# Moving the sample tile to the front of a hybrid decoder layer, routing each tile as it is finished, and adding the residual in the expert stage

## The reference

```
proj = x @ w_in
A half: causal conv + silu on q, k, v; gated delta rule in chunks over a state (per head 128x128); gated RMSNorm
B half: trailing means over 2/4/8/16 positions, a linear map per group
mix = concat(A, B) @ w_out ; h = LayerNorm(ALPHA*x + mix)
lg, le = h @ w_rg, h @ w_re               # 4 groups, 8 experts in each
top-1 group, top-2 experts in it, softmax weights
y = LayerNorm(ALPHA*h + sum over chosen experts of weight * (silu(h Wg) * (h Wu)) Wd)
```

## Time and profile before

| | us |
|---|---|
| device time, median of 3 runs | 1169.77 (1169.17 to 1171.09) |
| the profiled execution, its device time | 1168.77 |
| its span | 1167.0 |
| PE busy | 971.8 |
| DVE busy | 393.2 |
| ACT busy | 173.5 |
| POOL busy | 226.7 |
| stage 2, mixing, begins | 342 |
| stage 3, routing, begins | 712 |
| stage 4, experts, begins | 756.15 |
| stage 5, last LayerNorm, begins | 1108.5 |

### The profile page before, as it was taken

One profiled execution on the slowest core, in us unless ns is written; L12 is line 12 of the kernel. 1 busy time (PEld: TensorE's weight loads), 2 busy tenths in 40 slices (PEclk: granted clock), 3 DMA queues, 4 the chain that ended last, 5 costly groups with the idle time before them and its releaser, 6 DMA issues. The chain is left out here.

```text
span 1167.0 us, 13262 instructions
## 1 busy us (share of the span) xinstructions
PE 971.8 (83%) x5403; PEld 547.1 (47%) x5403; DVE 393.2 (34%) x737; ACT 173.5 (15%) x357; POOL 226.7 (19%) x238
## 2 busy tenths in 40 slices
PE   6999999999887999999988762049999999995583
PEld 4666666655445666666765422023333333331231
DVE  0434332586005554545542344201111111110056
ACT  1222233111021111111100000011111111110012
POOL 1011111220013222221113100611121211201047
PEclk9999999999888999999998875569999999998787
DMA  6011110202425011110031007757999999996094
GB/s 259 19 37 37 37 37 32 61 34 56 142 76 184 10 46 37 45 45 31 24 112 51 28 1 279 276 161 291 378 422 418 414 411 387 395 391 235 0 332 163
DMA packets 61323, 186.51 MB, mean 160 GB/s; under 512 B 22984, under 2 KB 36328, under 8 KB 51720
## 3 DMA queue, kind: packets, MB, share of 16 engines
q1 hardware_dynamic: 34640, 157.73, 35.3%
q0 software_dynamic: 8208, 19.09, 4.4%
q10 hardware_dynamic: 18416, 8.86, 2.7%
HBM read 164.15 MB, written 30.01 MB: 166 GB/s over the span
## 5 line engine op out<-in xcount | busy, mean ns | idle before, releaser
L359 PE MATMUL pj<-xT,wblk 128*128 128x384 f32 (+1 forms) x960 | 300.0, 474 | 18.3 <-DMA xT<-in_xt_dram 9.2
L359 PEld LDWEIGHTS pj<-xT,wblk 128*128 128x128 f32 x960 | 183.3, 192 | 129.8 <-issue 17.7
L1708 PE MATMUL e<-wgu_s,xgT 128*32 128x512 f32 x384 | 170.9, 598 | 0.0
L1708 PE MATMUL e<-wgu_a,xgT 128*32 128x512 f32 x768 | 114.7, 600 | 6.2 <-issue 3.2
L1708 PE MATMUL e<-wdn_a,acT 128*32 128x512 f32 x576 | 86.8, 592 | 0.7 <-ACT acT L1777 0.7
L1708 PE MATMUL e<-szT,acT 128*32 128x512 f32 x192 | 86.3, 592 | 0.0
L1694 PE MATMUL e<-cst,xg 128*128 128x128 f32 x200 | 28.7, 291 | 65.2 <-DMA xg<-h_dram,lst 48.4
L994 PE MATMUL b<-wout,yaT 128*128 128x512 f32 x144 | 69.7, 630 | 3.8 <-DVE yaT L1319 3.8
L1821 DVE SCALAR_TENSOR_TENSOR ac<-sg,lst,e 128x256 f32<-128x256 f32 x24 | 11.5, 480 | 171.2 <-ACT sg L1773 171.2
L1656 POOL DMA_INDIRECT picked_dram<-yo,lst x24 | 24.1, 1005 | 229.3 <-PE e L1694 185.0
L1708 PEld LDWEIGHTS e<-wgu_a,xgT 128*32 128x32 f32 x768 | 32.3, 111 | 75.9 <-issue 72.4
(11 more groups left out here) (321 smaller groups left out, 1248.4 us busy)
## 6 DMA issues: line engine op xcount, KB each, us to landing
wgu_a<-in_w_gate_up_dram SPq DMA_DIRECT2D x17, 2048.0 KB, 22.4
wdn_a<-in_w_down_dram SPq DMA_DIRECT2D x25, 1024.0 KB, 13.9
wgu_s<-in_w_gate_up_dram SPq DMA_DIRECT2D x8, 2048.0 KB, 15.6
qkvT<-in_w_gate_up_dram SPq DMA_DIRECT2D x8, 2048.0 KB, 19.4
wblk<-in_wcol_dram SPq DMA_DIRECT2D x20, 512.0 KB, 3.3
szT<-in_w_down_dram SPq DMA_DIRECT2D x8, 1024.0 KB, 18.1
picked<-picked_dram SPq DMA_DIRECT2D x8, 1024.0 KB, 5.7
h_dram<-h SPq DMA_DIRECT2D x9, 512.0 KB, 2.6
```

Source lines behind the costliest of these rows:

```text
L359: last = pe.matmul(pj[par][:, bank * 512:bank * 512 + m], wblk[par][:, k, :], xT[:, k, a:a + m], start=(k == 0), stop=(k == KT - 1))
L1708: last = pe.matmul(out[at, :], lhsT[:, at], theirs if j == GROUP - 1 else mine, start=start, stop=stop)
```

## The change

The tiles go in the order sample, prompt 0 to 7 (`ORDER`). The sample's states are loaded first, into rooms of their own (`st_s`); POOL scales them, and `sample_states` runs head by head in the second step, each with the same masked copy and the banks b3 and b4. Stage 3 goes: behind each tile's logits DVE chooses group and experts (`choose`), TensorE counts (`counts`) and DVE gives places (`place`) one step later, and POOL writes two scatters a tile. The weights of the expert stage are laid in the room of tiles that are finished, partly in steps 4, 7 and 9, and 12 MB behind the last product; the first gate/up slots are two in dead `qkvT` and three in turn. In stage 4 the gathered rows stay in four buffers (`NX = 4`) until the pass is put out, because `out_v` adds ALPHA times them, weighted by a fourth entry of the list; both halves are now DVE's. The order of overflow passes is worked out on DVE at pass 3. Stage 5 has no TensorE work: DVE adds the two rows, ACT takes the root, gain is split between DVE and POOL, bias is POOL's.

```diff
-            SAMPLE = PT
...
+            ORDER = [PT] + list(range(PT))
+            SAMPLE, LAST = 0, NT - 1
...
+                    for hh in range(H):
+                        sp.dma_start(st_s[hh], sdelta_d[0, :, hh].rearrange("s d e -> d s e")).then_inc(sst_in, 16)
+                    sp.dma_start(xct.rearrange("p n i -> p (n i)"), xct_d).then_inc(xc_in, 16)
+                    sp.dma_start(xc.rearrange("p n i -> p (n i)"), xc_d).then_inc(xc_in, 16)
...
+                        if i == 4:
+                            dead(3)
+                            load_own_gu(0)
...
+                            load_own_gu(1)
+                            e.wait_ge(ya_ready, 5)
+                            load_shared_dn(0)
+                        if a == LAST:
+                            dead(LAST)
+                            load_own_gu(2)
...
+                        if r == LAST:
+                            e.wait_ge(mix_done, NT)
+                            load_shared_gu(0)
+                            e.wait_ge(delta_out, 16)
+                            load_own_dn(0)
+                            load_own_dn(1)
+                            load_own_gu(3)
+                            load_own_dn(2)
+                            load_own_gu(4)
+                            load_shared_gu(1)
+                            load_shared_dn(1)
...
+                    pool.memset(on, 0.0).then_inc(cleared2, 1)
+                    pool.memset(xt[:, :], 0.0).then_inc(cleared2, 1)
+                    pool.memset(st, 0.0).then_inc(st_ready, 1)
...
+                        if a == SAMPLE:
+                            e.wait_ge(ks_raw, 1)
+                            for hh in range(H):
+                                pool.tensor_tensor(st_s[hh], st_s[hh], bc(eglast_s[:, :, hh], P), ALU.mult
+                                                   ).then_inc(scaled, 1)
...
+                        if r is not None and r >= 1:
+                            scatter(r - 1)
...
+                    scatter(LAST)
+                    e.wait_ge(listed, 16 * 2 * NT)
...
-                            if a < SAMPLE:
+                            if a == SAMPLE:
+                                sample_states(0)
+                            else:
...
+                        if a == SAMPLE:
+                            sample_states(1)
+                            mix(a, H + 2)
+                            sample_states(2)
+                            mix(a, H + 3)
+                            sample_states(3)
...
+                            if r >= 1:
+                                counts(r - 1)
...
-                        if a == SAMPLE:
-                            e.wait_ge(lg_ready, r + 1)
-                            for hh in range(H):
-                                sample_states(hh)
...
+                    e.wait_ge(lg_ready, NT)
+                    counts(LAST).then_inc(fixed, 1)
...
+                    def first_max(values, w, top, scratch, onehot):
+
+                        link(dve.tensor_reduce(top, values, AX.X, ALU.max))
+                        link(dve.scalar_tensor_tensor(out=scratch, in0=values, scalar=top, in1=w, op0=ALU.is_equal,
+                                                      op1=ALU.mult))
+                        link(dve.tensor_reduce(sm[:, :], scratch, AX.X, ALU.max))
+                        link(dve.tensor_scalar(onehot, scratch, sm[:, :], None, ALU.is_equal))
...
+                            if r >= 1:
+                                place(r - 1)
...
+                            choose(r)
...
-                        wait(e, xg_turned, q - 1)
-                        pool.indirect_dma_start(xg[q % 2][:, :], None, h_d,
+                        wait(e, yo_ready, 2 * (q - NX + 1))
...
-                    for q in range(3):
+                    for q in range(NX):
                         gather(q)
-                    for q in range(NPASS):
-                        if q + 3 < NPASS:
-                            gather(q + 3)
-                        if q >= 1:
-                            scatter(q - 1)
+                    for q in range(1, NPASS):
+                        scatter(q - 1)
+                        if q + NX - 1 < NPASS:
+                            gather(q + NX - 1)
...
-                def out_s(e, i, k):
-                    e.wait_ge(dn_done, i + 1)
-                    act.activation(yo[k][:, 0:512], b[6][:, :], ACT.Copy).then_inc(yo_ready, 1)
...
-                def out_v(e, i, k):
+                def out_v(e, i, k, rows, entry):
                     e.wait_ge(dn_done, i + 1)
-                    dve.tensor_copy(yo[k][:, 512:], b[7][:, :]).then_inc(yo_ready, 1)
+                    for half in range(2):
+                        c = slice(half * 512, (half + 1) * 512)
+                        dve.scalar_tensor_tensor(out=yo[k][:, c], in0=rows[:, c], scalar=entry.bitcast(F32),
+                                                 in1=b[6 + half][:, :], op0=ALU.mult, op1=ALU.add).then_inc(yo_ready, 1)
...
+                        if q == NA:
+                            overflow_order(e)
...
-            NB = 3
+            NB = 4
...
+                        pool.tensor_tensor(fin[k][:, hi], fin[k][:, hi], lng[:, hi], ALU.mult).then_inc(scaled_p, 1)
...
+                        pool.tensor_tensor(fin[k][:, :], fin[k][:, :], lnb[:, :], ALU.add).then_inc(out_ready, 1)
...
+                        dve.tensor_tensor(res[k][0:m, :], picked[k][0:m, 0:D], picked[k][0:m, D:], ALU.add
+                                          ).then_inc(summed, 1)
...
+                        dve.tensor_tensor(fin[k][:, lo], fin[k][:, lo], lng[:, lo], ALU.mult).then_inc(scaled_v, 1)
...
+                        link(dve.reciprocal(rstd[k][:, :], dev[k][:, :]))
+                        dve.scalar_tensor_tensor(out=shift[k][:, :], in0=mv[k][:, 0:1], scalar=-1.0, in1=rstd[k][:, :],
+                                                 op0=ALU.mult, op1=ALU.mult).then_inc(shift_ready, 1)
```

More of the change, by code:

```diff
@@ new lines, in build, with gu_rows, dn_rows @@
+        wdn_s = [dn_of(gates_of[:, k * DN:(k + 1) * DN]) for k in range(ND)]
+        kept = phase(whole)
+        gu_e_in = [kept(f"gu_e_in{k}") for k in range(EARLY)]
+        gu_a_in, dn_a_in = ([kept(f"{n}{i}") for i in range(NA)] for n in ("gu_a_in", "dn_a_in"))
+        gu_s_in, dn_s_in = ([kept(f"{n}{i}") for i in range(ND)] for n in ("gu_s_in", "dn_s_in"))
+        def gu_rows(expert):
+            return wgu_d[ds(expert, 1)].rearrange("a p k f -> (a p) k f")
+        def dn_rows(expert):
+            return wdn_d[ds(expert, 1)].rearrange("a p c d -> (a p) c d")
@@ L1024, in sample_states, with counts @@
                                              start=True, stop=True)
                         last.then_inc(ds_done, 1)
+                    def counts(r):
+                        e.wait_ge(both_ready, r + 1)
+                        pe.matmul(b[1][:, 64:64 + NE], C("strict"), both[:, :], start=True, stop=True)
+                        return pe.matmul(b[1][:, 64 + NE:64 + 2 * NE], C("ones"), both[:, :], start=True, stop=True)
                     def step(p, i, a, r):
-                        whole_tile = i is not None and i < SAMPLE
+                        whole_tile = i is not None and i != SAMPLE
@@ L1576, in build @@
+                            wait(e, gexp_ready, r)
+                            if r >= 1:
+                                place(r - 1)
+                            dve.tensor_tensor(logits[:, :], b[1][:, 0:G + NE], brt[:, :], ALU.add).then_inc(lg_ready, 1)
+                            e.wait_ge(lg_ready, r + 1)
+                            choose(r)
+                    steps(step)
+                    e.wait_ge(fixed, 1)
+                    place(LAST)
         with ExitStack() as c4:
@@ L1582, in build @@
             olst = sb("olst", [P, 4], I32, ctx=c4)
-            xg, xgT = two("xg", [P, D]), two("xgT", [P, KT, P])
+            NX = 4
+            xg = [sb(f"xg{k}", [P, D], ctx=c4)[:, :] for k in range(3)] + [rows_of[:, EARLY * GU:EARLY * GU + D]]
+            xgT = two("xgT", [P, KT, P])
             sg, ac, acT = two("sg", [P, FE]), two("ac", [P, FE]), two("acT", [P, FE // P, P])
```

883 lines of the change are left out of this document (395 added, 488 removed).

## The result

The changed kernel takes 1210.62 us (median of 4 runs, 1204.20 to 1213.87) against 1169.47 for the kernel before (measured once more, median of 4 now); the ratio is 1.0357, with a 95% interval of 1.0314 to 1.0401. That lies above the range given (1131 to 1192), and the likeliest case was no change. The profiled execution is the fastest of the four (1204.20, span 1202.4), so it is compared with the profiled execution of before (1168.77, span 1167.0): +35.4.

A forecast was written before the change was run, and what follows sets the result against it. TensorE was taken to bound mixing steps and expert passes, nearly idle from 712 to 778 us. Mixing, routing and start -42.5, passes +35.5, overflow residual +1.4, last stage +4 summed to -1.6: 1169.8 to 1168 us, range 1131 to 1192.

The forecast's parts named there:

- the likeliest case: Whole kernel: the forecast itself, sum -1.6 to 1168 us, own range 1158 to 1179, chance 0.35.
- (a): First two mixing steps: with the sample tile first no inverse to wait for, -10 of 10.7 us of waits.
- (b): Sample tile's second half: last step -17.8, state products behind it -13.0, second step +30 to 58 us; together -1.
- (c): Routing on DVE behind each step's logits: products taken 2.4 us late, mostly absorbed, +0.5 a step, +4 in all.
- The rival: Mixing steps: routing on DVE delays each step, the 2.4 us not absorbed, +15 over the sum, 1183 us; chance 0.10.
- the 36 that I had named as a sign of being wrong: Mixing steps: the prediction called itself wrong if steps run at 36 us.
- (d): Routing stage, last take to expert stage: 32.5 us instead of 62.45, -30; weights +1, bounds 0 and +8.
- (e): Start of the experts: first turn about 10 us after the stage begins instead of 16.4, -6.5, bounds 0 and -8.
- The expert passes: Gathers issued later with four buffers: light stalls 0.75, heavy 5.25 us, 42 less 6.5 of weight waits, +35.5.
- the lower clock behind them: Expert passes: stalls of 5 us may lower the clock, each costing up to 3 us; taken as 0, bound +18.
- The case that gathers land in time: Expert passes: a drained queue gives landings of 6.7 us, stalls 0 to 10 in all, 1133 to 1143 us; chance 0.25.
- The last stage: Sum without TensorE: first sum -6, POOL and DVE exclusion makes the period 5.4 us instead of 4.07, +10; net +4.

The follow-up runs named there:

- e_routing2: Changed kernel with group choice ahead of Y in the next step, expert choice at that step's end, scatters behind the next mask product: 1185.91 us, -24.7.
- e_five: Changed kernel with five buffers for gathered rows instead of four, so each gather is issued one pass earlier: 1168.00 us, -42.6.
- e_weightslate: Changed kernel, four buffers kept, with the next weights asked for only once POOL has issued the pass's gather: 1208.81 us, -1.8.
- e_last: Changed kernel's last stage with the sum on TensorE, whole gain on DVE, only bias on POOL, stores between loads: 1210.30 us, -0.3.
- e_shift: e_last with DVE's one-column shift using a scalar per row instead of a second tensor operand: 1202.13 us, -8.5 against the changed kernel.

## Why the prediction was wrong

**(a), (b) The sample tile first: right in the sum, 5 us too good, and in part by luck.** +20.7 to the first take against +20. The halves missed by 3 us each and cancelled: the first step lost 13.1 us (28.1 to 15.0), not 10, and the second took 61.2, not 58. In the second step the state rows' product alone took 10.6 us where 5 stood for it and its copy. In return, the row of 3.70 in the earlier trace rows holds the products of two heads and not of one, so the term 4 x 3.7 was counted twice; they took 10.1, partly at the lower clock, and the waits for DVE in it were 6.5 us, not 10.4. With routing out of the way (e_routing2) 267.5 us lie between the takes, against 293.8 - 17.8 - 13.0 = 263.0. By itself the new order of tiles brings -5.6 (20.7 - 26.3), where -11 stood.

**(c) Routing in each step: the step that failed.** "So the products are taken 2.4 us late. [...] I take +0.5 a step, +4 in all, bounds 0 and 8 x 2.4 = 19." It cost 26.2 us over the eight intervals (293.7 against 267.5). The lateness was 2.8 us, near the 2.4 by two errors: the operations are shorter than I took them (4.9 us without the long one, not 5.9), and the long one added 1.3. The steps ran at 38, beyond the 36 that I had named as a sign of being wrong. I asked whether DVE could make it up, and not who waits for the take: TensorE does, for banks b6 and b7, almost at once, and its wait of 3 us is followed by matmuls at the lower clock, so that the price is above the lateness itself: against e_routing2 TensorE is idle for 19.3 us more and busy for 6.9 more. Hence the bound of 19 was too low as well. The 1.3 us that one small operation lost beside POOL's mask product I had not priced, though I had read the same exclusion from the earlier trace rows for the last stage. The rival named this mechanism with 0.10 and at +15.

**(d), (e) Routing stage and start: right.** -27.6 against -29, and the first turn 9.1 us into the expert stage where 10 was said.

**The expert passes: the wait was right, the size by luck.** By e_five four buffers cost 39.1 us, against +35.5. But the waits sum to 33.4, not 42 (the long ones 4.3 to 5.8, as said; the light ones less), which leaves 26.9 us of idle time where 35.5 stood; and the lower clock behind them, which I had set to 0 with a bound of 18, cost 12.2. The two errors, 9 and 12 us, nearly cancel. The case that gathers land in time, to which I gave 0.25, fell. The earlier trace rows were the right rows; that a landing goes by the weights asked for just beside it was not shown: in e_weightslate it took 5.2 us 1.3 us ahead of 6 MB and 14.4 us 1.3 us ahead of 3.

**The last stage: right in mechanism, 3 us small.** +6.8 against +4: the first sum came 4.6 us earlier in the stage, not 6, and the rest was 11.3 longer, not 10, with tiles 5.7 and 5.0 us apart where 5.4 was said. The rule of the Trainium skill ("SBUF — State Buffer", Who interferes with whom) that POOL and a DVE operation with two SBUF inputs lock each other out agrees with e_last and e_shift, 2.33 against 0.21 us for the same column.

With 26 in place of 4 in (c) the sum is 1190, just inside the range, so (c) is the largest miss and not the whole of it. What is left in the five lines of the table, short by 1 to 5 us each and all to the same side, is some 15 us together, and by 5.7 more the changed kernel's median lies further above its profiled execution than the median of before.

## What to carry to other kernels

When work is put behind an operation on one engine, look up what the next operation of that engine frees, and for whom: idle time later in the loop gives nothing back to an engine that waits at that point. A buffer that is kept longer moves the issue of the transfer into it; compare the new lead with the landing time under the load of that moment, and try one more buffer first. In a stretch where GpSimd works, write small VectorE operations with a scalar per row instead of a second tensor.

## What the runs showed that I had not expected

The exclusion doesn't care for size: one column cost 2.33 us.

From the stage's first product to the first take, the profiled executions of the changed kernel and its variants, which share this code, took either 76.2 to 76.7 us (five of them) or 79.2 to 79.5 (six). The difference is in the products of the state rows, 64 records of matmuls with 16 moving columns. Windows of the changed kernel:

```profile
356.00:359.50 3.50, 2.64 (x13) 2.64 (x14) 0.00 (x0) 2.03 (x6) 3.50 (x6) 0.53 1.03 413
359.50:363.00 3.50, 3.50 (x33) 3.50 (x33) 3.28 (x3) 0.00 (x0) 3.28 (x2) 0.99 1.03 421
363.00:370.00 7.00, 7.00 (x35) 7.00 (x34) 1.11 (x3) 0.00 (x0) 0.00 (x0) 0.50 0.95 292
```

TensorE was busy without a gap, and the granted clock went from 0.99 to 0.50 in the middle of them, with these narrow matmuls the only work; 16 then take 3.5 us instead of 1.9. In the run with five buffers it was at 0.50 from before the first of them to the last, and the first 32 took 6.7 us instead of 3.6.
